# Feed-forward projections of a two-layer decoder step on one core: 512 prompt columns per product, 32 decode tokens in fp32 products of their own

## The reference

```python
a = rmsnorm(h, g_attn)
h = h + mix(split_columns(a @ w_in)) @ w_out      # three attention and pooling groups
h = h + conv_ffn(rmsnorm(h, g_ffn))[0]
h = h + sigmoid(rmsnorm(h, g_ple) @ w_ple_gate) * (p @ w_ple_proj)
```

```python
def conv_ffn(f, gate_prefix, w_up, conv_w, conv_b, w_down):
    up = f @ w_up                                  # (T, 1024) @ (1024, 5632)
    gate, val = up[..., :D_FF], up[..., D_FF:]     # D_FF = 2816
    g_ext = concatenate([gate_prefix, gate], axis=1)
    conv = conv_b + sum(g_ext[:, j:j + T] * conv_w[j] for j in range(3))   # causal, over tokens
    y = (silu(conv) * val) @ w_down                # (T, 2816) @ (2816, 1024)
    return y, g_ext[:, -2:]
```

## Times and profile before

| | |
|---|---|
| median of 3 runs | 1618.79 us (1617.92 to 1618.98) |
| profiled execution, own time | 1622.25 us |
| its span in the trace | 1620.5 us |
| PE busy | 1559.6 us, 96% |
| DVE, ACT, POOL busy | 882.3, 681.4, 276.6 us |
| up loop of the first layer on PE | 342.2 to 610.8 us |
| down of the first layer on PE | 610.8 to 745.3 us |

### The profile page before, as it was taken

The page is one execution under the profiler, slowest core; times in us unless marked ns, Lnnn a source line. Parts: engine busy times, 40 slices in busy tenths (PEclk is TensorE's granted clock), DMA queues, the critical chain, the costliest instruction groups (busy, mean ns, idle before and its releaser), DMA issues.

```text
span 1620.5 us, 30687 instructions
## 1 busy us (share of the span) xinstructions
PE 1559.6 (96%) x11808; PEld 1423.2 (88%) x11808; DVE 882.3 (54%) x1532; ACT 681.4 (42%) x989; POOL 276.6 (17%) x474
## 2 busy tenths in 40 slices
PE   6999979999999999999999999899999999999998
PEld 5887746999999999999978876479999999999997
DVE  6668884245555553223838688634455555522335
ACT  4344556244444442224443355543544444322241
POOL 3420350111111110100115204302111111101000
PEclk8999999999999999999999999999999999999999
DMA  5133144123333223322223411342232333322221
GB/s 178 53 99 88 33 142 110 53 66 91 91 89 90 80 87 100 92 82 84 79 79 83 117 46 48 103 109 79 79 91 79 90 90 88 100 85 83 87 79 61
DMA packets 225719, 140.24 MB, mean 87 GB/s; under 512 B 13122, under 2 KB 219604, under 8 KB 225552
## 3 DMA queue, kind: packets, MB, share of 16 engines
q1 hardware_dynamic: 223220, 133.46, 28.6%
q0 software_dynamic: 2400, 5.42, 1.1%
HBM read 131.21 MB, written 7.65 MB: 86 GB/s over the span
## 4 chain that ended last, share of the span: by engine, by line
PE 78%; DVE 13%; issue 3%; ACT 3%; POOL 1%; SPq 0%; DMA 0%; DVEq 0%; ACTq 0%; POOLq 0%
PE ps L1688 23%; PE ps L1690 23%; PE ps L1689 23%; DVE score L1354 3%; DVE m L1351 3%; DVE w_L L1253 2%; PE ps L2018 1%; PE ps L1947 1%; DVE Lb L1426 1%; PE ps L1715 1%; PE ps L1858 1%; PE ps L2102 1%; DVE stat L1473 1%; PE ps L1860 1%; DVE score L1338 0%
## 5 line engine op out<-in xcount | busy, mean ns | idle before, releaser
L1253 DVE TENSOR_TENSOR w_L<-w_raw,w_H 128x1024 fp32r<-128x1024 f32 (+4 forms) x236 | 257.7, 1101 | 419.2 <-ACT w_H L882 418.3
L1688 PE MATMUL ps<-bH,w_H 128*128 128x272 f32 x1664 | 481.0, 289 | 4.7 <-DVE w_L L1253 3.2
L1690 PE MATMUL ps<-bH,w_L 128*128 128x272 f32 x1664 | 479.5, 288 | 0.0
L1689 PE MATMUL ps<-bL,w_H 128*128 128x272 f32 x1664 | 477.8, 287 | 0.0
L882 ACT ACTIVATE w_H<-w_raw 128x1024 fp32r<-128x1024 f32 (+4 forms) x236 | 220.1, 944 | 282.4 <-PE ps L1690 281.7
L1688 PEld LDWEIGHTS ps<-bH,w_H 128*128 128x128 f32 x1664 | 312.6, 188 | 6.3 <-DVE w_L L1253 4.1
L1689 PEld LDWEIGHTS ps<-bL,w_H 128*128 128x128 f32 x1664 | 313.5, 188 | 0.1
L1690 PEld LDWEIGHTS ps<-bH,w_L 128*128 128x128 f32 x1664 | 312.6, 188 | 0.0
L1688 PE MATMUL ps<-actH,w_H 128*128 128x272 f32 x704 | 204.2, 290 | 0.0
L1690 PE MATMUL ps<-actH,w_L 128*128 128x272 f32 x704 | 203.7, 289 | 0.0
L1689 PE MATMUL ps<-actL,w_H 128*128 128x272 f32 x704 | 202.7, 288 | 0.0
(11 more groups left out here) (337 smaller groups left out, 2289.4 us busy)
## 6 DMA issues: line engine op xcount, KB each, us to landing
w_raw<-in_w_up SPq DMA_DIRECT2D x88, 512.0 KB, 3.8
w_raw<-in_w_down SPq DMA_DIRECT2D x32, 512.0 KB, 3.9
w_raw<-in_w_in SPq DMA_DIRECT2D x24, 512.0 KB, 4.6
w_raw<-in_w_ple_gate SPq DMA_DIRECT2D x16, 512.0 KB, 3.8
w_raw<-in_w_down SPq DMA_DIRECT2D x16, 384.0 KB, 3.3
w_raw<-in_w_out SPq DMA_DIRECT2D x16, 320.0 KB, 3.5
w_raw<-in_w_in SPq DMA_DIRECT2D x8, 452.0 KB, 4.1
w_raw<-in_w_in SPq DMA_DIRECT2D x8, 384.0 KB, 3.2
```

The source lines that it names most:

```text
L1253: ins = dve.tensor_tensor(w_L[u % SPLIT][:, a:b], w_raw[raw_slot(l, u)][:, a:b], w_H[u % SPLIT][:, a:b].bitcast(F32), ALU.subtract)
L1688: pe.matmul(out, wh, xh, start=start, stop=False)
L1689: pe.matmul(out, wh, xl, start=False, stop=False)
L1690: return pe.matmul(out, wl, xh, start=False, stop=stop)
```

## The change

In the two feed-forward projections the prompt and the decode tokens go apart. `prompt_dense` multiplies the 512 prompt columns in one product per pass (24 matmuls a unit of 8 blocks), in one bank a unit. The decode tokens (32 columns) are the stationary operand of plain fp32 matmuls against the unsplit weights in `w_raw`: 128 weight columns stream through, and the result has tokens on 32 partitions, so four such products go to the four column quarters of the array (PSUM partitions 0, 32, 64, 96). In the up loop the quarters are the four units of a turn (`up_decode`, 32 matmuls); ACT copies the 128 x 128 result from PSUM (`x_part`, semaphore `x_cp`), and PE transposes it back (`up_turn`, semaphore `up_dec`). In down the quarters are partial sums over blocks of one unit; after the third unit ACT copies them, and a product with a 0/1 matrix adds the quarters and transposes. The input `xs` (residual times gain) is made by one more DVE instruction; the norm factor is applied to the result as before. Raw slots now come free only when the decode product has read them too (`w_dec`), which SyncE waits for. Some semaphores elsewhere are merged under new names, without an effect on order.

```diff
@@ SyncE
                 with sp.Fori(0, KF // 2) as i:
+                    sp.wait_ge(w_dec, at(w_dec, i + 1))
+                    hold(sp)
                     for j in range(4):
                         load_unit(U_UP + j, i, 4)
...
                 for u in range(U_DOWN + RAW, UNITS + (RAW if l + 1 < LAYERS else 0)):
+                    if u < U_PROJ + RAW:
+                        sp.wait_ge(w_dec, at(w_dec, KF // 2 + 1 + u - U_DOWN - RAW + 1))
+                        hold(sp)
                     load_unit(u)
@@ ScalarE
-                    copy(act_at(actH, f), a_tmp[:, slot, :]).then_inc(f_hi, 1)
+                    copy(act_at(actH, f), a_tmp[:, slot, 0:TP]).then_inc(f_hi, 1)
...
                 with act.Fori(0, KF // 2) as i:
+                    act.wait_ge(w_dec, at(w_dec, i + 2))
+                    copy(x_part[:, :], ps[:, UP_PART, 0:P]).then_inc(x_cp, 1)
                     for j in range(2):
                         ffn(j, 2 * i + j, j, 2 * j, i, 4)
...
                         split(U_DOWN + 3 * m + q + 2)
+                        if q == 1:
+                            act.wait_ge(w_dec, at(w_dec, KF // 2 + 1 + 3 * m + 3))
+                            copy(x_part[:, :], ps[:, DOWN_PART, 0:P]).then_inc(x_cp, 1)
@@ VectorE
+                dve.wait_ge(h_new, at(h_new, 2 * KD))
+                dve.tensor_tensor(xs[:, :, :], hT[:, :, TP:T],
+                                  vecT[l][:, V_FFN:V_FFN + KD].unsqueeze(2).to_broadcast([P, KD, TS]), ALU.mult)
                 norm_low(1, KD - 1)
...
-                    dve.tensor_tensor(G[:, slot, 2:2 + HALF], ps[:, b, 0:HALF], r_all[:, 0:HALF], ALU.mult)
-                    dve.tensor_tensor(G[:, slot, 2 + HALF:2 + TP], ps[:, b + 1, 0:TP - HALF], r_all[:, HALF:TP], ALU.mult)
-                    dve.tensor_tensor(g_s[:, :, 2:6], ps[:, b + 1, TP - HALF:HALF].rearrange("p (b s) -> p b s", s=NS),
+                    dve.tensor_tensor(G[:, slot, 2:2 + TP], ps[:, b, :], r_all[:, 0:TP], ALU.mult)
+                    dve.wait_ge(up_dec, at(up_dec, i + 1))
+                    dve.tensor_tensor(g_s[:, :, 2:6], ps[:, UP_DEC, 64 * slot:64 * slot + TS].rearrange("p (b s) -> p b s", s=NS),
...
-                    dve.tensor_tensor(halves(a_tmp[:, slot, :]), halves(Cr[:, slot, :]), psh(4 * slot + 2), ALU.mult).then_inc(v_mul, 1)
+                    dve.tensor_tensor(act_at(xa, f), Cr[:, slot, TP:T], ps[:, UP_DEC, 64 * slot + TS:64 * slot + 2 * TS], ALU.mult)
+                    dve.tensor_tensor(a_tmp[:, slot, 0:TP], Cr[:, slot, 0:TP], ps[:, b + 1, :], ALU.mult).then_inc(v_mul, 1)
...
-                    dve.tensor_tensor(halves(hT[:, m, :]), halves(hT[:, m, :]), psh(DOWN_BANK[m % 4]), ALU.add).then_inc(h_new, 1)
+                    dve.tensor_tensor(hT[:, m, 0:TP], hT[:, m, 0:TP], ps[:, DOWN_BANK[m % 4], :], ALU.add)
+                    dve.tensor_tensor(hT[:, m, TP:T], hT[:, m, TP:T], ps[:, DOWN_DEC, 0:TS], ALU.add).then_inc(h_new, 1)
@@ TensorE
+                def prompt_dense(bank, u, blocks, xH, xL, first, last, norm_=None):
+
+                    H, Lo = w_H[u % SPLIT], w_L[u % SPLIT]
+                    for n, k in enumerate(blocks):
+                        if norm_ is not None:
+                            pe.wait_ge(a_lo, at(a_lo, 8 * norm_ + k + 1))
+                        w = slice(P * n, P * n + P)
+                        mm = tri_product(ps[:, bank, :], H[:, w], Lo[:, w], xH[:, k, 0:TP], xL[:, k, 0:TP],
+                                         first and n == 0, last and n == len(blocks) - 1)
+                    return mm
...
+                def up_decode(i):
+
+                    for j in range(4):
+                        slot = raw_slot(l, U_UP + j)
+                        pe.wait_ge(w_ld[slot], 16 * i + ld_value(l, U_UP + j))
+                        hold(pe)
+                    for k in range(KD):
+                        for j in range(4):
+                            mm = pe.matmul(ps[TS * j:TS * j + TS, UP_PART, 0:P], xs[:, k, :], w_raw[raw_slot(l, U_UP + j)][:, P * k:P * k + P],
+                                           start=k == 0, stop=k == KD - 1, skip_group_check=True)
+                    mm.then_inc(w_dec, 1)
+
+                def up_turn(i, first):
+
+                    pe.wait_ge(x_cp, at(x_cp, i + 1))
+                    if not first:
+                        pe.wait_ge(v_mul, at(v_mul, 2 * i + 2))
+                    pe.transpose(ps[:, UP_DEC, 0:P], x_part[:, :], ident).then_inc(up_dec, 1)
+
                 def up(i, first=False):
 
+                    if not first:
+                        up_decode(i)
                     for j in range(4):
...
-                        dense(2 * j, j, range(KD), bH, bL, True, True, norm_=1 if first and j == 0 else None).then_inc(w_used, 1)
+                        prompt_dense(j, j, range(KD), bH, bL, True, True, norm_=1 if first and j == 0 else None).then_inc(w_used, 1)
                         if first and j == 0:
+                            up_decode(0)
                             square_sum(1)
+                        if j == (1 if first else 0):
+                            up_turn(i, first)
...
-                        dense(DOWN_BANK[m % 4], u, range(8 * q, 8 * q + DOWN_K[q]), actH, actL, q == 0, q == 2).then_inc(w_used, 1)
+                        raw = w_raw[raw_slot(l, u)]
+                        for n in range(DOWN_K[q]):
+                            j = n % 4
+                            mm = pe.matmul(ps[TS * j:TS * j + TS, DOWN_PART, 0:P], xa[:, 8 * q + n, :], raw[:, P * n:P * n + P],
+                                           start=q == 0 and n < 4, stop=True, skip_group_check=True)
+                        mm.then_inc(w_dec, 1)
+                        mm = prompt_dense(DOWN_BANK[m % 4], u, range(8 * q, 8 * q + DOWN_K[q]), actH, actL, q == 0, q == 2)
+                        if q == 2:
+                            pe.wait_ge(x_cp, at(x_cp, KF // 2 + m + 1))
+                            if m >= 1:
+                                pe.wait_ge(h_new, at(h_new, 2 * KD + m))
+                            mm = pe.matmul(ps[:, DOWN_DEC, 0:TS], x_part[:, :], con[:, C_SUM:C_SUM + TS], start=True, stop=True)
+                        mm.then_inc(w_used, 1)
```

More of the change, by code:

```diff
@@ L263, in build @@
         ffn = ExitStack()
-        actH = sb("actH", [P, KF, T], F32R, ffn)
+        actH = sb("actH", [P, KF, TP], F32R, ffn)
         act_low = ExitStack()
-        sb("act_skip", [P, KF * T - DFF + 256], F32, act_low)
+        sb("act_skip", [P, KF * T + KF * TS - DFF + 256], F32, act_low)
         st_tok = sb("st_tok", [2 * NB, DFF], F32, act_low)
         act_low.close()
-        actL = sb("actL", [P, KF, T], F32R, ffn)
+        actL = sb("actL", [P, KF, TP], F32R, ffn)
+        xa = sb("xa", [P, KF, TS], F32, ffn)
+        xs = sb("xs", [P, KD, TS], F32, ffn)
+        x_part = sb("x_part", [P, P], F32, ffn)
+        sb("ffn_skip", [P, KF * TS - KD * TS - P], F32, ffn)
         keepT = sb("keepT", [P, KF, 2 + 2 * NB], F32, ffn)
@@ L367, in build @@
         SUM_BANK = [6, 6, 2]
+        UP_PART, UP_DEC, DOWN_PART, DOWN_DEC = 4, 5, 7, 5
         PP_BANK, PROJ_BANK = [2, 3, 1], [0, 4, 6]
@@ L659, in _ @@
             for t in range(TILES):
-                sp.wait_ge(y_ev, 2 * t + 2)
+                sp.wait_ge(rows_ev, 2 + 2 * t + 2)
                 if t < 4:
@@ L1232, in _ @@
                     i, n = 2 * t + b, TOKW[t]
-                    dve.wait_ge(emb_tr, i + 1)
+                    dve.wait_ge(rows_tr, i + 1)
                     ins = dve.tensor_copy(hT[:, 4 * b:4 * b + 4, P * t:P * t + n],
                                           ps[:, i % 8, :].rearrange("p (k q) -> p k q", q=P)[:, :, 0:n])
-                    ins.then_inc((emb_ev if i < 2 else h_new), 1)
+                    ins.then_inc((rows_ev if i < 2 else h_new), 1)
             dve.wait_ge(con_cast, 16)
@@ L1581, in ffn @@
                     split(U_UP + uo + 2, i, 4)
-                    b = 4 * slot
+                    b = 2 * slot
                     g_s = G[:, slot, 2 + TP:].rearrange("p (b s) -> p b s", s=6)
@@ L1603, in ffn @@
                     dve.wait_ge(w_used, at(w_used, 2 * f + U_UP + 1 + SPLIT + 1))
-                    dve.tensor_tensor(halves(a_tmp[:, slot, :]), halves(Cr[:, slot, :]), psh(4 * slot + 2), ALU.mult).then_inc(v_mul, 1)
+                    dve.tensor_tensor(act_at(xa, f), Cr[:, slot, TP:T], ps[:, UP_DEC, 64 * slot + TS:64 * slot + 2 * TS], ALU.mult)
+                    dve.tensor_tensor(a_tmp[:, slot, 0:TP], Cr[:, slot, 0:TP], ps[:, b + 1, :], ALU.mult).then_inc(v_mul, 1)
                     dve.wait_ge(f_hi, at(f_hi, f + 1))
-                    lo(act_at(actL, f), a_tmp[:, slot, :], act_at(actH, f)).then_inc(f_lo, 1)
+                    lo(act_at(actL, f), a_tmp[:, slot, 0:TP], act_at(actH, f)).then_inc(f_lo, 1)
                 with dve.Fori(0, KF // 2) as i:
@@ L1662, in _ @@
                 t, b, n = i // 2, i % 2, TOKW[i // 2]
-                dve.wait_ge(y_tr, i + 1)
```

(6 more changed lines are left out.)

25 lines of the change are left out of this document (12 added, 13 removed).

## The result

| | before | after |
|---|---|---|
| median | 1618.47 us (4 runs) | 1650.27 us (1648.22 to 1651.07, 4 runs) |
| ratio | 1 | 1.0196, 95% interval 1.0184 to 1.0209 |
| profiled execution, own time | 1622.25 us | 1651.07 us |
| its span | 1620.5 us | 1649.3 us |
| up, first layer, on PE | 268.6 us | 277.4 us |

The change costs 31.8 us. I had said 1628.5, range 1606 to 1645: the direction is right, the size is off by a factor of three, and the time lies outside the range.

The account below looks back on a forecast made before the run. PE bounded up, the ACT/DVE/POOL chain close behind; afterwards a loop through ScalarE's copy. Up 4.2, down 0.6 + 0.1: 4.9 us a layer, 9.8 for two, on 1618.8 gives 1628.6, say 1628.5; range 1606 to 1645.

Parts of the forecast that it names:

- The bound of before: Up turn before: PE's 192 matmuls 24.06 us, chain over ACT, DVE and POOL 23.6 by itself.
- The decode products: Up and down: fp32 quarter products at 0.028 us each, 0.11 a wave of four, 0.88 for 32.
- The 9 us: Whole forecast: growth of the sum if fp32 takes four passes, a wave 0.21 us and not 0.11.
- The whole products: Up and down: one matmul of 512 columns takes 0.231 us, against 0.2506 to 0.252 for two halves.
- A: Up and down: 512 columns cost 0.216 us, turn bounded by the chain at 23.75; 1599 us, chance 0.13.
- B: Up and down: loop closes tighter, whole matmuls at 0.226, turn 24.1; 1617.5 us, no change, chance 0.17.
- The loop through ScalarE's copy: Later up turns: PE's second unit awaits the copy, whose preceding split needs PE's third unit; 24.33 us a turn.
- The switches: Up and down: PE going from whole-array to quarter products and back costs 0.22 us together, ends 0 and 0.6.
- The first turn: Start of up: norm factor 0.75 us later, first split of slot 1 moves from 365.45 to 366.35.
- The loads: Raw weight slots in up and down: later release costs nothing, with 3.5 us to spare in up.
- C: Up and down: quarter products don't rotate, 0.11 us each; 1687 us, 1650 for half; with D chance 0.10.
- D: Whole change: halves weren't the cost, only the additions remain, within C's upper side; with C chance 0.10.

Follow-up runs that it names:

- one wave: Changed kernel with decode products cut to four per up turn (of 32) and four per down unit, rest of the decode sum left out: 1636.39 us.
- down's decode batched: Changed kernel with all 22 decode products of a down block issued together ahead of its third unit: 1642.70 us.
- 2 x 256: Changed kernel with the 512 prompt columns multiplied as two products of 256 into halves of the same bank: 1657.91 us.

## Why the prediction was wrong, and where it was right

**The bound of before: right.** PE at 24.06 and a chain at 23.6 a turn. The chain showed itself at 23.57 us a turn as soon as PE and the loop were out of its way.

**The decode products: wrong, and this is the step that failed.** I took 32 records, "x8" and "x24", for 32 products, and got 0.028 us for each. They are 16 products: the code at lines 2027 and 2029 issues 4 and 12 of them on each call, and I did not count them against the trace. 0.90/16 = 0.056 was there to be read, and the runs measured 0.055. The check of it by the first row, "three whole fp32 products" of 0.108, went wrong in the same way: these come from line 2018, which issues transposes, and a transpose is one record (as are the 22 of `x_part`), while a product is two. In the sum: in up 32 x 0.027 = 0.87 us a turn, in down 0.65 a block (and that with six waves, as I had them), in the first turn 0.9. For down that is 5.2 of the 6.7 us a layer by which it came out above the forecast.
The Trainium skill, "FP8 and Floating Point Precision", TensorE Precision Notes, says that true fp32 takes four passes through the array. I set it against that row and dismissed it. By this rule 128 columns are an estimated 4 x 128/2.4 = 213 ns whole and 53 on one of four quarters, and the trace agrees: 0.0547 us, and a wave of four such products (0.219 us) is 3.8 times a wave of bf16 ones (0.057). The 9 us that I had attached to the rule were too few as well: PE's turn rises by 0.87 to 24.4 and, with whole products at 0.234, to 24.7, over the loop's 24.33. Ten turns of 0.35, 0.9 in the first and 5.2 in down are 9.6 us a layer, 19 in all, and 1628.5 + 19 = 1647.5 is within 3 us of what was measured.

**The whole products: nearly right.** 0.230 in down against my 0.231; in up 0.234, which makes 0.3 us a turn. Rivals A (0.216) and B (0.226) are out: the mean spacing is at neither in either stage.

**The loop through ScalarE's copy: the right mechanism in second place.** With one wave it appeared at 24.56, each of its two parts as I had them within 0.2 us. In the changed kernel PE's own 24.68 covers it in every turn but the second. I had set PE's own work at 23.5 and so the loop on top. That up came out slower, as I had said, is therefore luck: without this loop my own terms put the turn at 23.75 and up about 1 us faster than before, and what made it slower is PE's own work. Bounds of a turn that lie within 1 us of each other are only as good as the price of the largest count in each.

**The switches: mis-sized, small.** 0.33 in up for my 0.22; in down 0.24 to 0.31. The summing product takes 0.23 us and not 0.15; it is two records as well. In down a block is 66 x 0.230 + 6 x 0.219 + 3 x 0.29 + 0.23 = 17.6, which is the whole of it; my 16.72 lacks 0.65 (products), 0.2 (switches) and 0.1 (sum).

**The first turn: right but for the same price.** From the start of up to the first split of slot 1 took 25.19 us, 1.98 more than before; I had 0.90. Of the missing 1.1, 0.87 are the decode products ahead of the sum of squares: with seven of their eight waves left out (one wave) it took 23.66 us, 1.53 less, and 28 x 0.0547 is 1.53.

**The loads: right.** In up and down of the changed kernel nothing waits for a DMA, nor where the slots are held longest (down's decode batched).

**The rivals.** C had the right effect, a higher price in up and down with PE as the bound, and its mild form stood at 1650. It had a wrong reason, that the quarters do not rotate: they do, four in flight, at the price of an fp32 product. D, that the halves were not the cost, was right in up, where splitting costs nothing (2 x 256); the saving a pair came all the same, from the 32 columns that left it. I gave C and D together 0.10.

## What to carry to other kernels

Before a price is read from a group of records, count the instructions in the code that made them: here an fp32 product is two records and a transpose one. Where columns are taken out of a stream, their price in it is columns times the time of one (32 x 0.46 ns = 0.015 us a pass, 0.35 us a unit of 24 passes), and whatever replaces them has to be cheaper than that: eight fp32 quarter products are 0.44 us before any switch, bf16 ones 0.11. And when several bounds lie close together, give each its own uncertainty, since the one that is named first may be the second.

## What the runs showed of the hardware

An fp32 matmul appears as two pairs of weight load and matmul, on four column quarters 0.0547 us a product of 128 columns; in bf16 it is one pair and 0.014 us. An fp32 transpose is one pair. A half wave (two of four quarters) costs as much as a whole one. Two fp32r products of 256 columns cost what one of 512 does in up (0.03 us for 96 extra instructions in a turn) and 0.006 us more in down. An fp32r product of 512 columns takes 0.234 us in up and 0.230 in down; why these differ was not settled. The change from whole to quarter products and back costs 0.24 to 0.33 us.
